# Streamed first projections: the GpSimd part moved to VectorE, two accumulation chains, q weights as row blocks, gate columns in four parts, a short bias-line table

## The reference, cut to what matters

```python
mod = jax.nn.silu(c) @ w_ada + b_ada                      # c: 1 x 1024, w_ada: 1024 x 3072
shift, scale, gate = jnp.split(mod, 3, axis=-1)
h = rms_norm(x, norm_gain) * (1 + scale[:, None, :]) + shift[:, None, :]
proj = h @ w_in                                           # w_in: 1024 x 3096
(q_a, k_a, v_a, z_a, q_b, kc, vc, ks, vs, kw, vw, z_b, g_b) = jnp.split(proj, _split_points(), axis=-1)
...
return x + gate[:, None, :] * out                         # at the end of the layer
```

## Time and profile before

| | us |
|---|---|
| median of 3 runs | 1547.82 |
| the profiled execution | 1547.39 |
| its span | 1545.7 |
| TensorE busy (matmuls) | 1480.8 |
| VectorE busy | 756.1 |
| ScalarE busy | 574.8 |
| GpSimd busy | 106.0 |

### The profile page before, as it was taken

How to read it: one execution, slowest core, us unless ns; L and a number is a source line. 1 busy time by engine, 2 the same in 40 slices (tenths; PEclk the granted TensorE clock), 3 DMA queues, 4 the chain that set the end, 5 groups by cost and what they waited for, 6 DMA issues and landing times.

```text
span 1545.7 us, 18106 instructions
## 1 busy us (share of the span) xinstructions
PE 1480.8 (96%) x6974; PEld 1229.5 (80%) x6974; DVE 756.1 (49%) x1181; ACT 574.8 (37%) x941; POOL 106.0 (7%) x92
## 2 busy tenths in 40 slices
PE   4798998999899999999999999999999999999998
PEld 3577887887788888888888878888878888888886
DVE  6833236776456653354643625555455633333332
ACT  2332334655343333233333334443344433333221
POOL 4310310000000000001000023210000000000000
PEclk7898899999999999999999999999999999999998
DMA  8877410000243333331222222325332333333321
GB/s 237 236 232 177 123 55 28 1 1 1 62 157 104 87 109 95 95 109 42 82 75 61 82 68 82 96 82 157 88 96 85 106 96 96 95 101 94 109 79 54
DMA packets 242557, 148.27 MB, mean 96 GB/s; under 512 B 22338, under 2 KB 232490, under 8 KB 242224
## 3 DMA queue, kind: packets, MB, share of 16 engines
q1 hardware_dynamic: 239216, 131.90, 30.1%
q0 software_dynamic: 3264, 15.32, 3.0%
HBM read 138.82 MB, written 7.34 MB: 95 GB/s over the span
## 4 chain that ended last, share of the span: by engine, by line
PE 66%; issue 24%; DVE 5%; DMA 3%; ACT 1%; SPq 0%; POOLq 0%; POOL 0%; DVEq 0%; ACTq 0%
PE ps L381 44%; PE ps L1821 6%; PE ps L1845 3%; PE ps L1741 3%; PE ps L1545 3%; PE ps L1755 2%; DMA w_raw<-in_w_in_dram 2%; DVE ada_sum L997 2%; PE ps L1831 1%; PE ps L1642 1%; PE ps L1605 1%; DMA w_ada_shift_scale<-in_w_ada_dram 1%; PE ps L1635 1%; PE ps L1577 1%; DVE h_lo L1021 0%
## 5 line engine op out<-in xcount | busy, mean ns | idle before, releaser
L401 DVE TENSOR_TENSOR w_lo<-w_raw,w_hi 128x1024 fp32r<-128x1024 f32 (+1 forms) x215 | 263.2, 1228 | 286.3 <-ACT w_hi L396 283.6
L396 ACT ACTIVATE w_hi<-w_raw 128x1024 fp32r<-128x1024 f32 (+1 forms) x223 | 228.8, 1034 | 51.2 <-DMA w_raw<-in_w_in_dram 38.3
L408 ACT ACTIVATE temps<-ps 128x512 f32<-128x512 f32 x68 | 40.6, 596 | 251.1 <-PE ps L381 251.1
L381 PE MATMUL ps<-g_hi,w_hi 128*128 128x512 f32 x384 | 97.5, 396 | 0.0
L381 PE MATMUL ps<-g_hi,w_lo 128*128 128x512 f32 x384 | 94.9, 389 | 0.0
L381 PE MATMUL ps<-g_lo,w_hi 128*128 128x512 f32 x384 | 94.8, 389 | 0.0
L381 PEld LDWEIGHTS ps<-g_hi,w_hi 128*128 128x128 f32 x384 | 71.6, 188 | 16.4 <-issue 1.9
L381 PEld LDWEIGHTS ps<-g_hi,w_lo 128*128 128x128 f32 x384 | 72.1, 188 | 15.1
L381 PEld LDWEIGHTS ps<-g_lo,w_hi 128*128 128x128 f32 x384 | 72.1, 188 | 15.0
L1755 PEld LDWEIGHTS ps<-proj,probs_t 128*128 128x128 f32 x432 | 61.5, 191 | 13.9 <-issue 7.6
L800 ACT ACTIVATE scores_sb<-scores_sb,row_min 128x256 f32<-128x256 f32 (+3 forms) x96 | 51.2, 533 | 54.2 <-DVE row_min L1191 53.0
(11 more groups left out here) (360 smaller groups left out, 2740.8 us busy)
## 6 DMA issues: line engine op xcount, KB each, us to landing
w_raw<-in_w_in_dram SPq DMA_DIRECT2D x99, 512.0 KB, 3.8
w_raw<-in_w_ff_gate_dram SPq DMA_DIRECT2D x22, 512.0 KB, 3.8
w_raw<-in_w_ff_up_dram SPq DMA_DIRECT2D x22, 512.0 KB, 3.8
w_ada_shift_scale<-in_w_ada_dram SPq DMA_DIRECT2D x16, 512.0 KB, 6.6
...
```

The lines of the kernel that those rows point to most:

```text
L381: mm = pe.matmul(bank, w[:, slot, k], mov[:, at_k], start=first and n == 0 and k == 0, stop=last and n == 2 and k == kts - 1)
L396: act.activation(whi[:, slot, 0:kts], raw[:, slot, 0:kts], ACT.Copy).then_inc(hi_done, 1)
L401: nc.vector.tensor_tensor(wlo[:, slot, 0:kts], raw[:, slot, 0:kts], whi[:, slot, 0:kts].bitcast(F32), ALU.subtract).then_inc(lo_done, 1)
L408: act.activation(dst, ps[:, o % 4], func, scale=scale).then_inc(evac, 1)
```

## The change

1. **GpSimd leaves the stream.** `x_rstd` and the subtraction for `w_lo` of units 0 to 7 go to VectorE, in line with its other steps.
2. **Two accumulation chains.** `ada_sum` has two accumulators; steps k = 0, 2, 4, 6 go into one and k = 1, 3, 5, 7 into the other, so each step waits for the one before the last. There are 2 products and 6 multiply-adds for each tile. TensorE adds the two up in PSUM, 4 one-column matmuls in place of 2. `mod_sums(u + 1)` moves from between the first and second pass of unit u to between the second and third.
3. **Start.** The first `w_ada` loads are issued ahead of x, the sum for tile 0 is made ahead of the sums of squares, the first `w_hi` conversion moves behind the third x tile on ScalarE, `mod_sums(0)` ahead of the 1/rms broadcast on TensorE.
4. **q weights as row blocks.** A q unit is now 256 rows by 512 columns, one load of 2 KB runs. Four units add into four banks (4 to 7, then 0 to 3); the 4 tiles are copied out together behind the fourth. The conversions put the heads in order, in two halves of 512 each.
5. **Gate columns in four parts** of 1 MB, in two buffers, behind q units 0, 2, 4, 6. The one-column sums move behind the last q unit, and `mod` (gate) with them.
6. **16 bias-line rows.** The line is written 16 times, not 128, and as soon as it is there. `band_a` and `band_b` are read in 16 loads of 16 partitions each in place of 2 of 128.

```diff
+            def heads_of(t, u, kk, order):
+                return half_rows(t, u)[:, kk].rearrange(f"p ({order} d) -> p j g d", g=2, j=4)
...
-            sp.dma_start(ada_g[:], w_ada_v[:, 0:4, 2048:3072]).then_inc(m["adag_in"], 16)
             for n in range(8):
-                u, a = U_Q + n, Q_COLS[n // 4] + (n % 4) * HD
-                load_pair(u, r[:, :, 0:HD], r[:, :, HD:P], w_in_v[:, :, a:a + HD],
-                          w_in_v[:, :, a + 4 * HD:a + 5 * HD])
...
+                a, c2 = Q_COLS[n // 4], n % 4
+                load_rows(U_Q + n, w_in_v[:, 2 * c2:2 * c2 + 2, a:a + 512])
+                if n % 2 == 0:
+                    rows2 = n // 2
+                    if rows2 >= 2:
+                        sp.wait_ge(m["adag_done"], rows2 - 1)
+                    sp.dma_start(ada_g[:, rows2 % 2], w_ada_v[:, n:n + 2, 2048:3072]).then_inc(ada_in[rows2], 16)
...
-            pool.wait_ge(m["row_done"], 1)
-            for k in range(KT):
-                pool.wait_ge(m["x_ev"], max(X_ORDER.index(j) for j in range(k + 1)) + 1)
-                g.tensor_tensor(x_r[:, k], x_t[:, k], rs_row[:], ALU.mult).then_inc(m["xr_done"], 1)
-                pool.wait_ge(hi_done, k + 1)
-                g.tensor_tensor(wlo[:, k % SLOTS, 0:ROW_OUTS], raw[:, k % SLOTS, 0:ROW_OUTS],
-                                whi[:, k % SLOTS, 0:ROW_OUTS].bitcast(F32), ALU.subtract).then_inc(lo_done, 1)
...
-            pool.dma_start(band_a[:], bass.AP(line_dram.tensor, 127, skew)).then_inc(m["band_in"], 16)
-            pool.dma_start(band_b[:, :, 256:512],
-                           bass.AP(line_dram.tensor, 8 * LINE + 127, skew)).then_inc(m["band_in"], 16)
+            skew = [[16 * LINE - 1, 16], [LINE, 8], [1, 256]]
+            for a in range(0, P, 16):
+                for q, band in enumerate((band_a, band_b[:, :, 256:512])):
+                    pool.dma_start(band[a:a + 16], bass.AP(line_dram.tensor, 8 * q * LINE + 127 - a,
+                                                           skew)).then_inc(m["band_in"], 16)
...
+            def ada_sum(u, ks):
+                if ks[0] == 0:
+                    dve.wait_ge(ada_in[u % 4], 32 * (u // 4 + 1))
+                    if u >= 2:
+                        dve.wait_ge(m["mod_mm"], u - 1)
+                for k in ks:
+                    dst, src = acc[:, u % 2, k % 2], ada[:, u % 4, k]
+                    if k < 2:
+                        v.tensor_scalar(dst, src, csilu[:, k:k + 1], None, ALU.mult).then_inc(m["ada_step"], 1)
+                        continue
+                    dve.wait_ge(m["ada_step"], 7 * u + k - 1)
+                    v.scalar_tensor_tensor(out=dst, in0=src, scalar=csilu[:, k:k + 1], in1=dst, op0=ALU.mult,
+                                           op1=ALU.add).then_inc(m["ada_step" if k < KT - 1 else "ada_done"], 1)
...
             for u in range(KT):
-                modulation(u)
-                if u < KT - 1:
-                    ada_sum(u + 1, range(4))
+                if u:
+                    modulation(u)
+                    if u < KT - 1:
+                        ada_sum(u + 1, range(4))
                 dve.wait_ge(m["th_done"], u + 1)
                 v.tensor_tensor(h_lo[:, u], t_h[:, u % 2], h_hi[:, u].bitcast(F32), ALU.subtract).then_inc(m["hl_done"], 1)
+                if u and u < KT - 1:
+                    ada_sum(u + 1, range(4, KT))
                 if u < KT - 1:
-                    ada_sum(u + 1, range(4, KT))
+                    x_rstd(u + 1)
+                dve_convert(dve, None, 0, u + 2, ROW_OUTS if u + 2 < KT else KT)
...
+            dve.wait_ge(m["modg_mm"], 1)
+            own(v.tensor_tensor(mod[:, 16:24], ps[:, 6, 0:8], col[:, V_ADA + 16:V_ADA + 24], ALU.add))
...
+                for j in range(4):
+                    for n, (w, h) in enumerate(((whi, h_hi), (wlo, h_hi), (whi, h_lo))):
+                        for kk in range(2):
+                            mm = pe.matmul(ps[:, 4 - 4 * q + j], half_rows(w, u)[:, kk, blk(j)], h[:, 2 * c2 + kk],
+                                           start=c2 == 0 and n == 0 and kk == 0, stop=c2 == 3 and n == 2 and kk == 1)
...
+            for u in range(U_Q, U_Z):
+                q_unit(u)
+            pe.wait_ge(evac, 12)
+            pe.wait_ge(m["adag_done"], 4)
+            column_sums(6, acc_g, 8).then_inc(m["modg_mm"], 1)
```

More of the change, by code:

```diff
@@ L386, in loads_of @@
         def loads_of(u):
-            paired = len([n for n in range(u % SLOTS, u + 1, SLOTS) if U_Q <= n < U_Z])
-            return u // SLOTS + 1 + paired
+            return u // SLOTS + 1
         def act_convert(act, it, per, u, kts=KT):
@@ L452, in _, with load_ada @@
                 sp.dma_start(vec[first:first + n, :], src.rearrange("a (m p) -> (a m) p", p=P)).then_inc(m["vec_in"], 16)
+            def load_ada(u):
+                for part in range(2):
+                    n = part * D + u * P
+                    sp.dma_start(ada[:, u % 4, :, part], w_ada_v[:, :, n:n + P]).then_inc(ada_in[u % 4], 16)
+            load_ada(0)
             x_v = x[0].rearrange("(i p) d -> p i d", p=P)
@@ L486, in _ @@
                     sp.wait_ge(m["ada_done"], u - 3)
-                for part in range(2):
-                    n = part * D + u * P
-                    sp.dma_start(ada[:, u % 4, :, part], w_ada_v[:, :, n:n + P]).then_inc(ada_in[u % 4], 16)
+                if u:
+                    load_ada(u)
                 if u >= SLOTS:
@@ L712, in _ @@
                     a.activation(rs_row[:], ps[:, 7], ACT.Copy).then_inc(m["row_done"], 1)
+                if n == 2:
+                    act_convert(act, None, 0, 0, ROW_OUTS)
             act_convert(act, None, 0, 1, ROW_OUTS)
@@ L732, in _ @@
                 a.activation(proj[:, o], ps[:, o], ACT.Copy).then_inc(evac, 1)
-            for o in range(ROW_OUTS, 16):
-                act_convert(act, None, 0, o + U_OF + AHEAD)
-                act_out(act, None, 0, o + U_OF, proj[:, o], o, ACT.Copy)
+            for u in range(U_KA, U_Z):
+                convert_at(act_convert, act_convert_q, act, u + AHEAD)
+                if u < U_Q:
+                    act_out(act, None, 0, u, proj[:, u - 2], u - 2, ACT.Copy)
+                q, c2 = divmod(u - U_Q, 4)
+                if u >= U_Q and c2 == 3:
+                    for j in range(4):
+                        act.wait_ge(m["kv_mm"] if j < 3 else unit_done, ROW_OUTS + 3 * q + j if j < 3 else u + 1)
+                        a.activation(proj[:, QA + 4 * q + j], ps[:, 4 - 4 * q + j], ACT.Copy).then_inc(evac, 1)
             def square_head(t):
@@ L1039, in _ @@
                     own(v.tensor_scalar(gains[:, 2:6], col[:, V_GAIN + 2:V_GAIN + 6], -1.0, None, ALU.mult))
-                half = {8: 0, 9: 1, 11: 2, 12: 3}.get(o)
-                if half is not None:
-                    for k in (2 * half, 2 * half + 1):
-                        if k % 4 == 0:
-                            dve.wait_ge(m["adag_in"], 16 * (k // 4 + 1))
+                c = {U_Q + 1: 0, U_Q + 2: 1, U_Q + 4: 2, U_Q + 6: 3}.get(u)
+                if c is not None:
+                    dve.wait_ge(ada_in[c], 64 + 16)
+                    for k in (2 * c, 2 * c + 1):
+                        src = ada_g[:, c % 2, k % 2]
                         if k == 0:
-                            own(v.tensor_scalar(acc_g[:], ada_g[:, 0], csilu[:, 0:1], None, ALU.mult))
+                            own(v.tensor_scalar(acc_g[:], src, csilu[:, 0:1], None, ALU.mult))
                             continue
-                        if k == 4:
-                            dve.wait_ge(m["adag_done"], 1)
                         own.wait()
-                        ins = v.scalar_tensor_tensor(out=acc_g[:], in0=ada_g[:, k % 4], scalar=csilu[:, k:k + 1],
+                        if k and k % 2 == 0:
+                            dve.wait_ge(m["adag_done"], c)
+                        ins = v.scalar_tensor_tensor(out=acc_g[:], in0=src, scalar=csilu[:, k:k + 1],
                                                      in1=acc_g[:], op0=ALU.mult, op1=ALU.add)
-                        if k % 4 < 3:
+                        if k % 2 == 0:
                             own(ins)
@@ L1573, in rows_bc, with column_sums @@
                 return mm
-            def column_sums(bank, src, n, first=0, at_col=0):
+            def column_sums(bank, src, n, first=0):
                 for q in range(n):
-                    mm = pe.matmul(ps[:, bank, at_col + q:at_col + q + 1], src[:, blk(first + q)], ones1[:],
+                    mm = pe.matmul(ps[:, bank, q:q + 1], src[:, blk(first + q)], ones1[:],
                                    start=True, stop=True)
@@ L1582, in mod_sums @@
                 pe.wait_ge(m["ada_done"], u + 1)
-                sums = acc[:, u % 2].rearrange("p a n -> p (a n)")
-                column_sums(6, sums, 2, at_col=448 + 2 * u).then_inc(m["mod_mm"], 1)
+                for part in range(2):
+                    for half in range(2):
```

(5 more changed lines are left out.)

118 lines of the change are left out of this document (59 added, 59 removed).

## The result

The changed kernel takes 1535.53 us (median of 6 runs, 1534.36 to 1537.59) beside 1547.11 us before (6 runs, 1542.05 to 1547.95): the ratio is 0.9935, with an interval of 0.9917 to 0.9953. It is faster by 0.65%, or 11.6 us; the forecast was 1.4%, and 1535.5 lies just above the range of 1518 to 1534. The profiled run took 1534.36 us (span 1532.6, mean granted clock 0.981).

The account below looks back on a forecast made before the run. VectorE's modulation sums bound the stream, TensorE nearly everything else. Saving 13.7 us in the stream plus the waits in units 8 to 17, less a 3.2 us hole and 1.7 us of clock, gave 21.9 us: 1525.7 us, range 1518 to 1534.

Parts of the forecast that it names:

- the low clock behind the new hole: Behind the gate sums, at the compressed MLP: clock low after a 3.2 us hole, costing 1.7 us, bounds 0 and 3.4.
- The wait for tile 4's rows: In the stream: small loads keep SyncE until 34.43, tile 4's rows land near 41; 0.5 us added (0 to 2).
- The start: Start of the kernel: TensorE's first pass 1.0 us later, at 23.8 in place of 22.80, bounds -1 and +3.4.
- t(1): Start of VectorE's bias step for tile 1 in the stream, forecast at 30.8 us.
- A tile's step: In the stream: 5.89 us per tile on VectorE, multiply-adds 0.41 apart in place of 0.52, TensorE's work hidden.
- Units 8 to 17: After the stream: 10 units at 5.44 us, 54.4 us in all, both weight waits and their clock loss gone.
- GpSimd's queue: 16 band issues at 0.88 us, 14.1 us in all; `shifted` lands at 99, wanted at 130.7, 31 us of cover.
- A: Rival, in the stream: the second chain doesn't pay, four steps stay at 0.52, 2.6 us more, 1528.3 us; chance 0.10.
- B: Rival: no low clock behind the new hole, and a quicker stream with the clock up in tile 0, 1521 to 1524; chance 0.10.
- C: Rival, q loads: they stay late and both weight waits return, 8.3 + 3.4 us, 1537.4 us; chance 0.07.
- D: Rival, in the stream: TensorE is held at the lower clock, 10.4 us a tile, 1557 us, slower than before; chance 0.04.
- E: Rival, band loads: the narrow loads go one after another, `shifted` comes 50 us late, 1576 us; chance 0.02.

## Why the prediction was wrong, point by point

- **The step that failed: the low clock behind the new hole.** I foresaw the hole (3.2 us; it is 3.33) and that the clock would be low behind it, and took 1.7 us, bounds 0 to 3.4, from the hole before a q unit. It cost 7.7 against the kernel before. That price was read where 512-column passes follow; here 64-column matmuls follow, and they don't bring the clock back, whether for their width or their kind. The kernel with eight wide matmuls in between, the one with the hole filled and the kernel before with the hole put in all show it. That is 6.0 of the 8.9 us between 1525.5 and the profiled 1534.36.
- **The wait for tile 4's rows: 2.3 us of the rest.** I had seen that the small loads hold SyncE until 34.43 and added 0.5 us, bounds 0 to 2. They held it until 36.22, the tile's step was 8.70 instead of the 6.4 forecast, and the next step 6.80 instead of 5.9 for the clock behind it; the clean tiles, 0.2 us faster each than forecast, gave 0.9 back. Most of it was the wait itself, 3.0 us over a clean step of 5.67 where I had 0.5; the clock behind it, 1.1, I hadn't priced at all.
- **The start**: t(1) was 30.89, forecast 30.8, and so close by luck, as errors cancelled. The first pass was 1.0 us late (24.80, within the bounds), but the column sums came 5.1 us behind it (29.91) instead of 5.6 and took 1.0.
- **A tile's step**: 5.67 instead of 5.89, VectorE setting the pace, 0.40 against 0.41 for a multiply-add; this was the mechanism forecast. From the last bias step to the first k/v pass 76.69 - 69.32 = 7.37 against 7.41. With the tile-4 wait, 76.69 in place of 74.4, 11.4 us saved instead of 13.7.
- **Units 8 to 17**: 54.5 us against 54.4, both waits and their clock loss gone, as forecast. ScalarE did wait 12.2 us for one q block, until 107.86, and the block before covered it.
- **GpSimd's queue**: the 16 band issues took 0.53 us each instead of 0.88, each landed some 17 us after its issue, and nothing waited for them or for `shifted` (issued from 82.2, landed 19 to 21 us after).
- **The rivals**: A fell in the trace (0.40 against 0.52), though the time can't tell. B didn't come in either part: the clock was low behind the hole, and the first passes of tile 0 ran at the low clock (2.90 us for six matmuls). C, D and E didn't come either. None of them had the right mechanism, and the range's upper end had no room for it.
- **Two slips in the prediction that changed little**: the mean clock of 0.93 belongs to the units 8 to 17, not to later stages as I used it for the range; and D and E together had 0.06, more than the 0.05 I gave to "slower".

What stays open is why the pieces of 2-column matmuls bring the clock down while the 64-column MLP, at full clock, does not; the runs show only that it is so.
